# Low parts written over the loaded weight tiles, four high parts, and four tiles held at the end of a down projection

## The reference, cut to what matters

```python
x = layer_norm(ALPHA * x + mix, ln1_g[l], ln1_b[l])
ffn = (jax.nn.silu(x @ w_ffn_gate[l]) * (x @ w_ffn_up[l])) @ w_ffn_down[l]
x = layer_norm(ALPHA * x + ffn, ln2_g[l], ln2_b[l])
...
x = x + mixed @ w_o[layer]
h = rmsnorm(x, ffn_norm[layer])
x = x + conv_ffn(h, w_up[layer], conv_w[layer], conv_b[layer], w_down[layer])
```

## Time and profile before

| | |
|---|---|
| median of 3 runs | 1466.06 us (1465.76 to 1473.11) |
| the profiled execution's own time | 1465.25 us |
| its span | 1463.5 us |
| mean granted TensorE clock | 0.978 of full speed |
| PE busy | 1389.7 us, 95% |
| DVE busy | 976.4 us, 67% |
| ACT busy | 700.4 us, 48% |
| moved by DMA | 233.22 MB, 159 GB/s over the span |

### The profile page before, as it was taken

The page is one execution under the profiler, slowest core; times in us unless marked ns, Lnnn a source line. Parts: engine busy times, 40 slices in busy tenths (PEclk is TensorE's granted clock), DMA queues, the critical chain, the costliest instruction groups (busy, mean ns, idle before and its releaser), DMA issues.

```text
span 1463.5 us, 24482 instructions
## 1 busy us (share of the span) xinstructions
PE 1389.7 (95%) x10006; PEld 1285.3 (88%) x10006; DVE 976.4 (67%) x1660; ACT 700.4 (48%) x1149; POOL 85.1 (6%) x79
## 2 busy tenths in 40 slices
PE   9998899999999898999998999999999999999997
PEld 7997689999899777999987998889998899889996
DVE  5766775555759466655565685787768555786777
ACT  4755444334385543434344544455545454454453
POOL 0320000000014000000000011120000000000000
PEclk9999999999999899999998999999999999999999
DMA  8742245555443213655533434345454433445441
GB/s 317 276 150 87 87 147 195 177 192 183 166 155 137 91 59 121 225 175 195 178 131 142 145 116 145 134 163 183 180 200 159 173 123 132 157 157 206 187 173 58
DMA packets 38343, 233.22 MB, mean 159 GB/s; under 512 B 4984, under 2 KB 8776, under 8 KB 11864
## 3 DMA queue, kind: packets, MB, share of 16 engines
q1 hardware_dynamic: 36168, 224.18, 43.2%
q0 software_dynamic: 2064, 7.47, 1.6%
HBM read 230.55 MB, written 1.09 MB: 158 GB/s over the span
## 4 chain that ended last, share of the span: by engine, by line
PE 82%; DVE 10%; ACT 4%; issue 2%; POOL 0%; DMA 0%; SPq 0%; DVEq 0%; ACTq 0%
PE bank L746 24%; PE bank L747 24%; PE bank L748 23%; DVE w_lo L582 2%; PE bank L850 2%; ACT w_hi L572 1%; PE bank L930 1%; PE bank L952 1%; PE bank L954 1%; PE bank L953 1%; DVE a_lo L603 1%; DVE nstat L1555 1%; PE bank L826 1%; DVE arena L1630 0%; ACT a_hi L598 0%
## 5 line engine op out<-in xcount | busy, mean ns | idle before, releaser
L582 DVE TENSOR_TENSOR w_lo<-raw,w_hi 128x1024 fp32r<-128x1024 f32 x404 | 484.9, 1237 | 97.4 <-ACT w_hi L572 94.2
L746 PE MATMUL bank<-a_hi,w_hi 128*128 128x256 f32 x1856 | 530.0, 286 | 3.1 <-DVE w_lo L582 3.1
L747 PE MATMUL bank<-a_lo,w_hi 128*128 128x256 f32 x1856 | 525.9, 283 | 0.0
L748 PE MATMUL bank<-a_hi,w_lo 128*128 128x256 f32 x1856 | 525.8, 283 | 0.0
L572 ACT ACTIVATE w_hi<-raw 128x1024 fp32r<-128x1024 f32 x404 | 406.3, 1050 | 97.6 <-PE bank L748 89.6
L746 PEld LDWEIGHTS bank<-a_hi,w_hi 128*128 128x128 f32 x1856 | 356.4, 192 | 7.4 <-issue 4.4
L747 PEld LDWEIGHTS bank<-a_lo,w_hi 128*128 128x128 f32 x1856 | 356.5, 192 | 1.3
L748 PEld LDWEIGHTS bank<-a_hi,w_lo 128*128 128x128 f32 x1856 | 356.6, 192 | 0.0
L746 PE MATMUL bank<-w_hi,a_hi 128*128 128x256 f32 (+1 forms) x512 | 168.8, 330 | 16.3 <-DVE a_lo L603 15.5
L747 PE MATMUL bank<-w_lo,a_hi 128*128 128x256 f32 (+1 forms) x512 | 161.8, 316 | 0.0
L748 PE MATMUL bank<-w_hi,a_lo 128*128 128x256 f32 (+1 forms) x512 | 161.3, 315 | 0.0
(11 more groups left out here) (248 smaller groups left out, 1484.4 us busy)
## 6 DMA issues: line engine op xcount, KB each, us to landing
raw<-in_stream SPq DMA_DIRECT2D x201, 1024.0 KB, 4.9
bias_t<-bias_rows SPq DMA_DIRECT2D x6, 512.0 KB, 7.0
heads_buf<-in_w SPq DMA_DIRECT2D x2, 1024.0 KB, 7.9
gains<-in_w SPq DMA_DIRECT2D x2, 1024.0 KB, 10.0
gains<-in_ln_g POOLq DMA_DIRECT2D x4, 512.0 KB, 3.9
gains<-in_ln_b POOLq DMA_DIRECT2D x4, 512.0 KB, 5.7
gains<-in_rms_g POOLq DMA_DIRECT2D x3, 512.0 KB, 3.8
res<-in_xT SPq DMA_DIRECT2D x4, 256.0 KB, 5.2
```

What stands on the lines that cost most here:

```text
L582: dve.tensor_tensor(w_lo[:, i % PARTS, half_tile(h)], raw[:, i % SLOTS, half_tile(h)], w_hi[:, i % PARTS, half_tile(h)].bitcast(F32), ALU. ...
L746: pe.matmul(out, lh, rh, start=first, stop=False)
L747: pe.matmul(out, lh, rl, start=False, stop=False)
L748: return pe.matmul(out, ll, rh, start=False, stop=last)
```

## The change

The tiles are loaded into buffers that the low part is then written over: `raw` and `w_lo` are the same memory now, five buffers deep (`SLOTS` = 5 in place of 3). `w_hi` has four buffers (`PARTS` = 4 in place of 3). With that,

- the load of tile i waits until PE has used tile i-5, where before it waited until tile i-3 was split;
- the high part of tile i waits until tile i-4 is used and stands behind the work on tile i-4;
- the low part subtracts in place;
- four `down` tiles are held at the end (`down7` to `down10`, `TAIL` = 4), and `h_hi` and `h_lo` have eight columns (`HSLOTS` = 8);
- SP's first loads are issued without a wait up to tile 4, and the gain of one norm (`gain4`) lies elsewhere in the arena. The order of SP's transfers is the same.

```diff
-SLOTS = 3
+SLOTS = 5
-PARTS = 3
-HSLOTS = 6
+PARTS = 4
+HSLOTS = 8
-TAIL = 3
+TAIL = 4
...
-    return order + [("down", FT // 2 - 3 + i) for i in range(TAIL)]
+    return order + [("down", FT // 2 - TAIL + i) for i in range(TAIL)]
...
-        raw = sb("raw", [P, SLOTS, TILE])
+        with nc.sbuf_tensor("raw", [P, SLOTS, TILE], F32) as raw:
+            pass
+        w_lo = sb("w_lo", [P, SLOTS, TILE], F32R)
         w_hi = sb("w_hi", [P, PARTS, TILE], F32R)
-        w_lo = sb("w_lo", [P, PARTS, TILE], F32R)
...
-        gain4 = arena[:, 5120:5120 + D]
+        gain4 = arena[:, 6144:6144 + D]
...
-            dve.tensor_tensor(w_lo[:, i % PARTS, half_tile(h)], raw[:, i % SLOTS, half_tile(h)],
+            dve.tensor_tensor(w_lo[:, i % SLOTS, half_tile(h)], raw[:, i % SLOTS, half_tile(h)],
                               w_hi[:, i % PARTS, half_tile(h)].bitcast(F32), ALU.subtract).then_inc(w_lo_done, 1)
...
                 if i >= SLOTS:
-                    wait_split(sp, i - SLOTS)
+                    wait_used(sp, stream[i - SLOTS])
                 sp.dma_start(raw[:, i % SLOTS, :], a["stream"][i]).then_inc(tile_loaded[i % SLOTS], 16)
...
-            for i in range(1, SLOTS):
+            for i in range(1, 3):
                 load(i)
...
-            load(SLOTS)
-            load(SLOTS + 1)
+            load(3)
+            load(4)
...
-                return w_hi[:, i % PARTS, :], w_lo[:, i % PARTS, :]
+                return w_hi[:, i % PARTS, :], w_lo[:, i % SLOTS, :]
```

More of the change, by code:

```diff
@@ L698, in _ @@
                 sp.dma_start(dst, a[name]).then_inc(consts_in, 16)
-            load(SLOTS + 2)
-            load(SLOTS + 3)
+            load(5)
+            load(6)
             sp.wait_ge(bias_row_ready, 1)
             sp.dma_start(scratch, bias_row[0:24, :]).then_inc(rows_out, 16)
-            load(SLOTS + 4)
+            load(7)
             sp.wait_ge(rows_out, 16)
@@ L709, in _ @@
                 sp.dma_start(bias_t[:, heads, :], src).then_inc(bias_in, 16)
-                load(SLOTS + 5 + g)
+                load(8 + g)
                 if g == 0:
@@ L713, in _ @@
             sp.dma_start(x[:, :, :], a["x"]).then_inc(x_rows_in, 16)
-            load(SLOTS + 5 + BIAS_READS)
+            load(8 + BIAS_READS)
             sp.dma_start(conv_col[:, :, :, :], a["conv_col"]).then_inc(x_rows_in, 16)
-            for i in range(SLOTS + 6 + BIAS_READS, len(stream)):
+            for i in range(9 + BIAS_READS, len(stream)):
                 load(i)
```

## The result

The changed kernel took 1486.2 us (median of 4 runs, 1484.5 to 1491.7) beside 1468.5 us for the kernel before (4 runs, 1465.8 to 1473.1): 1.0126 times the time, 95% interval 1.010 to 1.0152, which is 15 to 22 us. That is slower, by 17.7 us where I had predicted 13.7 on a slightly lower base. The forecast of 1479.5 is 6.7 us under the measured median, and 2.4 of these come from the kernel before, whose median with more runs stands at 1468.5 in place of 1466.1. The result lies above my own range of 1475 to 1484 and inside the wider one of 1469 to 1487. The profiled execution of after has a span of 1482.8 us, 19.3 more than before, at a mean granted clock of 0.970 (before 0.978).

The account below looks back on a forecast made before the run. PE was taken as the bound, busy 1389.7 of 1463.5 us, so only its gaps could move the time. Ends 11.3 plus start 2.4 gave 13.7 us more, forecast 1479.5 us, own range 1475 to 1484, wider 1469 to 1487.

Parts of the forecast that it names:

- The ends of the layers: Late loads and an extra low split delay second-half norms in layers 0 to 2; layer 3 gains: 11.3 us in sum.
- The signs I named: Profile marks: two ACT DMA waits per end, paired low splits, no 0.97 us waits, SP waiting for PE.
- PE's late start on n0: End of layer 0: PE starts n0 1.8 us later, inside the same wait as the second half's norm.
- 4.5 us longer: Layer 0: PE's wait before the second half's transposes grows by 4.5 us.
- its root was, as I wrote, 2 us late: End of layer 1: the root behind n2's high part on ACT comes 2.1 us late.
- gaps of PE under 10 us more at the ends: Failure sign: the prediction fails if PE's gaps at layer ends grow by under 10 us in sum.
- Bounds 0 and 4; I take 2.4: Kernel start: tile 5's extra low split delays `start()` and the gates; cost 2.4 us, bounds 0 and 4.
- Layer 1's recurrence at 0: Layer 1's recurrence: the 3.1 us low-part wait goes, but DVE's chain ends the gain; 0, bounds -1 and +2.
- In-place writing and the steady run at nothing: Low splits keep their 1237 ns mean; steady feed-forward loads land 0.7 us before needed; cost nothing.
- Only the extra split counts: Rival: n1 and n2 land in time, each end costs 2.35 us; 1471 to 1473.5 us; chance 0.15.
- Late all along: Rival: steady-run loads land near 6 us, delaying `up` tiles in layers 2 and 3; 1490 us; chance 0.11.
- Not slower: Rival: the fourth held tile covers the norms, up to -12 us, more likely -5 (1461); chance 0.08.

Follow-up runs that it names:

- experiment 5: Changed kernel with n2's high part on ACT moved behind the transposed half's high parts, DVE's order kept: 1474.25 us, ratio 1.0043.
- Experiment 3: Changed kernel with DVE running `start()` ahead of tile 5's low split: 1478.28 us, ratio 1.0071.
- the two other pairs: Changed kernel with three held tiles, and with n2's splits later on ACT and DVE, each without and with `start()` sooner: 6.0 and 5.1 us apart.
- experiment 1: Changed kernel holding three `down` tiles in place of four: 1475.25 us, ratio 1.0043.
- experiment 4: Changed kernel with 14 to 44 unread identity matmuls ahead of transposes where PE waits, oversized: 1492.78 us, ratio 1.0164.
- experiment 2: Changed kernel with n2's high part behind the transposed half's on ACT and its low part behind the second half's norm on DVE: 1462.87 us, ratio 0.9961.
- experiment 6: Changed kernel with 7 to 22 unread identity matmuls, sized to the gaps, ahead of transposes where PE waits: 1475.2 us, ratio 1.0043.
- experiment 8: Changed kernel with six loaded tiles, three high-part buffers and three held tiles, low parts still in place: 1469.39 us, ratio 1.0012.
- both new orders: Changed kernel with n2's splits later on ACT and DVE and `start()` ahead of tile 5's low split: 1457.75 us, ratio 0.9927.

## Why the prediction was right and where it fell short

**The ends of the layers** were right in place, mechanism and size. The signs I named are there: two DMA waits of ACT at each of three ends, two low splits side by side between L604 and L1551, no wait of 0.97 in layers 2 and 3, SP waiting for PE. The lags are 4.31, 4.11 and 3.60 us and -1.3 in layer 3: 10.7 in sum where I had 11.3. Even the landings fit: ACT starts the high parts of n1 and n2 at 382.93 and 385.66, which is 375.8 and 378.6 of the prediction plus the 7.0 us that the kernel is late by there. (The figure of the Trainium skill in the prediction, from "DMA: Bandwidth & Descriptors", section "Anatomy of one DMA", is given there for transfers issued by GpSimd. These are issued by SP and took 4.8 us, and the sum did not use the figure.) Three details differ. First, PE's late start on n0, which I called part of the same wait, came as a wait of its own: in layer 0 the 4.3 us are 1.83 at n0's a_lo plus 2.3 more at the second transposes, so "4.5 us longer" at the latter was wrong while the sum held. Second, in layer 1 nothing was lost behind the second half by the late load; its root was, as I wrote, 2 us late, but PE paid for it at the first half's transposes (2.63 us of wait in place of 0.62); experiment 5 takes this away with ACT's order. Third, I had named gaps of PE under 10 us more at the ends as a sign of failure. They grew by 4.1, 3.2 and 2.9 us at three ends and lost 1.9 in layers 2 and 3, 8.3 in all. PE's matmuls in between ran at the lower clock for a while (0.58 in 1152 to 1156 us), which shortened its second wait, while DVE's chain still set the time. So the lag is the better measure, and the sign was set without the clock.

**The step that failed is the start: "Bounds 0 and 4; I take 2.4".** The delay itself was sized fairly. Tile 5's load let ACT go at 28.05 (I had estimated near 27), `start()` came at 31.42, 3.8 us late where I had 2.4 to 3, and PE's product 2.84 us late. But I ended the sum at PE's wait. That wait grew from 0.79 to 3.73 us, and behind it the clock was at 0.50, for another 2.5 us of lag. So the start cost 5.3 us in place of 2.4, more than my upper bound of 4. Experiment 3 and the two other pairs, which remove the delay, give back 5.1 to 7.9 us and not 2.4. My sum had no term for the granted clock, at the start or anywhere: it treated each us that PE waits as one us. With 5.3 and 10.7 the traces account for 16.0 us. The fall of the clock at 121.68 (another 1.6 us) is not part of this: the gap there is the same in all kernels, and the loss behind it goes with the single execution, not with the start.

By the Trainium skill ("TensorE: Matmul & The Clock Gate", section "Part 1: The HAM clock gate") the gate has two levels, follows how busy PE has lately been, and where it changes shifts from run to run. The trace agrees: windows of 4 us show 0.50, 1.00 or a mean between the two, and the traces differ behind equal gaps (1.00 behind 1.90 us in before, 0.73 behind 1.89 in after).

**How much of it is clock?** The runs themselves give an estimate. Among the 23 runs of before beside experiments 1 to 4, those at a mean clock of 0.979 took 1465.6 to 1466.2 us and those at 0.973 took 1471.1 to 1472.1: about 1 us for each 0.001, and the runs of experiments 1, 2, 5 and 6 have nearly the same slope. The mean over all runs is 0.976 for before and 0.969 for after. By this an estimated 7 of the 17.7 us go with the lower clock, the 2.5 behind the start among them. With the gaps at the norms filled the two kernels are 14.2 us apart, at mean clocks of 0.987 and 0.985. That fits roughly, but the 3.5 us less than 17.7 are inside the noise. The two profiled executions can't split such amounts: PE's time between 508 and 532 us was granted 0.80 before and 0.87 after, and between 532 and 560 it was 1.00 and 0.82.

**Layer 1's recurrence at 0** held in what I meant: the wait of 3.1 us for a low part went and came back as 0.34 + 2.58 us at the next product of the DVE chain. The +2.5 us in this stretch of the table is not explained by any wait, and other profiles of kernels with the same work there show 0.0 to -4.4 us, so it is not shown to be a cost of the change.

**In-place writing and the steady run at nothing** was right for PE (1239 ns; no new gap in the feed-forward runs; experiment 8). I had each load landing 0.7 us before ACT wants it, though, and ACT has 21 more waits for a load than before. Twelve of them lie away from the ends and the start, and they reach PE nowhere.

**The rivals.** "Only the extra split counts" is excluded by the DMA waits and by experiment 5. "Late all along" is excluded: a load takes 4.8 us, ACT waits for 3 loads around the beginning of the feed-forward parts of layers 2 and 3 and not for all 22, and PE has no new gap there. "Not slower" failed for the reason I gave, the hand-written order: experiment 2 changes this order and nothing else, and the kernel is faster than before.

**What stays open:** why experiments 1, 2, 3, 5 and 6 all gave back more than I expected. A low clock that goes with the longer waits fits: the mean clock is 0.975, 0.980, 0.973, 0.975 and 0.985 in their runs and 0.969 in after. But that the shorter waits are what raised it was shown at the start alone. Open is also how much more an order made for five and four buffers would give.

## What to carry to other kernels

When a change adds buffers, look at where the order of work is written out in terms of them: here one more tile ahead put one more split in front of a norm and of `start()`, and ACT's order put a late load in front of the transposed half. With the old order the change cost 1.3%; with those splits moved behind what PE waits for, the same buffers were worth 0.7%. Cost a wait that grows on PE at more than its length (at the start, waits of up to 1.8 us kept the clock and waits of 3.6 us and more lost it in every profile, while elsewhere gaps of 1.9 us lost it in some): look in the windows behind similar waits of the trace for what the clock did there, and add it as a term of its own. If such a gap can't be closed, matmuls that nobody reads can hold the clock, but they must be sized inside the gap by their measured time, and the kernel before must be filled as well before the gain is credited to anything else.

## What the runs showed of the hardware

- Filling PE's gaps with matmuls that nobody reads made two kernels faster: by 7.8 us (before, mean granted clock of the runs 0.976 to 0.987) and 11.0 us (after, 0.969 to 0.985). With both new orders it is 3.8 us (0.983 to 0.988), inside the noise.
- Runs of one kernel differ by their clock: 1465.6 to 1466.2 us at a mean of 0.979 and 1471.1 to 1472.1 at 0.973 (before).
- The same gap does not cost the same clock: PE waits 1.90 us at 116.34 in before and 1.89 us at 121.68 in after. Before has 1.00 in the windows 116 to 124 and 0.64 in 124 to 128, where PE is 58% busy; after has 0.73 in 120 to 124 and 0.84 in 124 to 128, where it is 94% busy.
- An f32 matmul of 128x128 by the identity is recorded as two of 0.12 us; counting one made the first filling twice too long, and the kernel 6.6 us slower (some of the filling also stood where no gap was).
- A subtraction that overwrites one of its own inputs took 1239 ns against 1237 into another buffer (404 of each).
